# A streaming encoder step on one core: the middle half of each MLP's down product made of seven products of sums instead of eight

## The chip, the cores and the metric

The kernel runs on one core of one Trainium2 chip. The metric is the device time of the program in microseconds. Its engines are TensorE (PE, with its weight loads as PEld), VectorE (DVE), ScalarE (ACT), GpSimd (POOL) and SyncE (SP), which issues the DMAs. Each engine runs its instructions in program order and waits on semaphores for the others.

## What is computed

Two layers over 1056 rows (1024 of a prompt, 32 of a running stream), model width 1024. Layer 0 mixes by spatial gating and a recurrence, layer 1 by a short gated convolution; after each mixer comes the MLP that is changed here:

```python
x = x + rmsnorm(m, p['norm_mix_post'][l])
hn = rmsnorm(x, p['norm_ffn_pre'][l])
f = jnp.square(jax.nn.relu(hn @ p['mlp_up'][l])) @ p['mlp_down'][l]
x = x + rmsnorm(f, p['norm_ffn_post'][l])
```

mlp_up is 1024 x 4096, mlp_down 4096 x 1024, all float32.

## The kernel before

Activations are held transposed: 128 partitions are 128 features, and the 1056 rows are columns, in NT = 3 tiles of TT = 352. A product in float32 is made of three fast matmuls. Each operand is split into a high part (a cast to the short form, on ACT) and a low part (raw minus high, on DVE), and a 128x352 result takes high x high, high weights x low data, low weights x high data, for each of 8 blocks of 128 features: 24 matmuls that accumulate in one PSUM bank (lines 698 to 700, in `unit`). Such a 24 is a *unit*; a *panel* is one load of weights, 1024 x 128, used in 3 units.

`plan` writes down the list of units and of loads. Weights come by SP's DMAs into three rotating places (w_all), each free again when the last unit that used it is done (SP waits on pe_unit). ACT's `high` (line 876) casts them and DVE's `low` (line 1183) subtracts, at the units that high_at and low_at give. 

The MLP runs in four groups. In a group, 8 up panels give 1024 of the 4096 hidden features: DVE's `evacuate` (line 1286) scales and rectifies a PSUM bank into one of three tmp tiles, ACT squares it (937) and casts it to h_hi (939), DVE subtracts into h_lo (`h_low`, 1266). Then 8 down panels multiply these with mlp_down, and DVE adds each bank to f in SBUF (line 1292; the first group's is a copy, 1289). Six PSUM banks go round, so a unit waits for the evacuation six units before. The two other banks (M0, M1) serve norms and transposes, and line 760 is such a small product between units. In the last group f is squared for the norm.

POOL works at the start and in layer 1's mixer (lines 654 to 664), and is idle in the MLPs.

## Time and profile before

| | us |
|---|---|
| median of 3 runs | 2157.8 |
| lowest, highest | 2157.34, 2158.69 |
| span of the profiled execution | 2155.1 |
| PE busy in it | 2146.0 |
| DVE busy | 908.0 |
| ACT busy | 652.9 |
| POOL busy | 100.1 |

The span is measured from the first to the last instruction of the profiled execution; the runs' times contain some 2.7 us more. A matmul's record is about twice as long as its share of PE's time, since the next one starts while it drains: PE's pace is read from starts, not from durations. Weight loads (PEld) overlap the matmuls in the same way.

### The profile page before, as it was taken

Reading aid. Unit: us, or ns where it says so; the run is one execution under the profiler, and the core shown is the slowest. Engines: PE = TensorE matmul, PEld = TensorE weight load, DVE = VectorE, ACT = ScalarE, POOL = GpSimd, SP = SyncE. Lnnn points to the kernel's source line nnn. Section 1 sums busy time; section 2 is a strip of 40 time slices with the busy share of each in tenths; the row PEclk is TensorE's granted clock in tenths of the full one; section 3 lists DMA queues with packets and bytes.
Section 4 is the critical chain, followed back from the end, with each engine's and each line's share of the span. In section 5 each row is a group of like instructions: output and inputs, shape, how many; then the busy total and the mean of one; then the engine's idle time right before and its main releaser. Section 6 shows DMA issues by size and latency. Waiting matters only on the chain.

```text
span 2155.1 us, 31488 instructions
## 1 busy us (share of the span) xinstructions
PE 2146.0 (100%) x13496; PEld 2135.0 (99%) x13496; DVE 908.0 (42%) x1414; ACT 652.9 (30%) x1105; POOL 100.1 (5%) x127
## 2 busy tenths in 40 slices
PE   9999999999999999999999999999999999999998
PEld 9999999999999999999999999999999999999998
DVE  8766367323322322334953333493223223322336
ACT  6673355202301310333511112453013103202332
POOL 2000000000000000000043231000000000000000
PEclk9999999999999999999999999999999999999999
DMA  5111422111111111141311114222111111111142
GB/s 165 35 41 40 139 88 72 50 40 49 50 42 47 49 50 40 49 135 44 120 50 47 43 50 139 67 84 59 42 48 50 49 40 50 50 42 48 50 140 81
DMA packets 208410, 138.65 MB, mean 64 GB/s; under 512 B 6000, under 2 KB 204784, under 8 KB 208272
## 3 DMA queue, kind: packets, MB, share of 16 engines
q1 hardware_dynamic: 207552, 135.51, 20.6%
q8 instruction: 107, 1.75, 0.3%
q10 hardware_dynamic: 720, 1.13, 0.1%
q14 instruction: 31, 0.25, 0.0%
HBM read 119.22 MB, written 17.40 MB: 63 GB/s over the span
## 4 chain that ended last, share of the span: by engine, by line
PE 99%; ACT 1%; DMA 0%; DVE 0%; issue 0%; DVEq 0%; ACTq 0%
PE ps L698 32%; PE ps L700 32%; PE ps L699 32%; PE ps L773 1%; PE ps L801 0%; PE ps L729 0%; PE ps L720 0%; DMA w_all_raw<-in_w_in_even_dram 0%; PE ps L716 0%; PE ps L784 0%; PE ps L760 0%; ACT L1074 0%; ACT L1030 0%; ACT lru L1030 0%; ACT lru L1032 0%; ACT gelu L1074 0%
## 5 line engine op out<-in xcount | busy, mean ns | idle before, releaser
L698 PE MATMUL ps<-x_hi,w_all 128*128 128x352 f32 x2304 | 747.0, 324 | 0.0
L700 PE MATMUL ps<-x_hi,w_all 128*128 128x352 f32 x2304 | 739.1, 321 | 0.0
L699 PE MATMUL ps<-x_lo,w_all 128*128 128x352 f32 x2304 | 739.1, 321 | 0.0
L698 PE MATMUL ps<-h_hi,w_all 128*128 128x352 f32 x1728 | 556.2, 322 | 0.0
L700 PE MATMUL ps<-h_hi,w_all 128*128 128x352 f32 x1728 | 555.2, 321 | 0.0
L699 PE MATMUL ps<-h_lo,w_all 128*128 128x352 f32 x1728 | 555.2, 321 | 0.0
L698 PEld LDWEIGHTS ps<-x_hi,w_all 128*128 128x128 f32 x2304 | 432.4, 188 | 2.7
L699 PEld LDWEIGHTS ps<-x_lo,w_all 128*128 128x128 f32 x2304 | 432.4, 188 | 2.2
L700 PEld LDWEIGHTS ps<-x_hi,w_all 128*128 128x128 f32 x2304 | 432.3, 188 | 0.0
L876 ACT CAST w_all<-w_all_raw 128x1024 fp32r<-128x1024 f32 x166 | 173.5, 1045 | 525.1 <-DMA w_all_raw<-in_mlp_down_dram 324.8
L698 PEld LDWEIGHTS ps<-h_hi,w_all 128*128 128x128 f32 x1728 | 324.5, 188 | 0.3 <-DVE h_lo L1452 0.3
L699 PEld LDWEIGHTS ps<-h_lo,w_all 128*128 128x128 f32 x1728 | 324.5, 188 | 0.0
L700 PEld LDWEIGHTS ps<-h_hi,w_all 128*128 128x128 f32 x1728 | 324.4, 188 | 0.0
L1286 DVE SCALAR_TENSOR_TENSOR tmp<-ps,rstd 128x352 f32<-128x352 f32 x192 | 100.3, 523 | 419.2 <-PE ps L700 419.0
L937 ACT ACTIVATE tmp<-tmp 128x352 f32<-128x352 f32 x192 | 95.7, 498 | 472.4 <-DVE tmp L1286 472.2
L1292 DVE TENSOR_TENSOR f<-ps,f 128x352 f32<-128x352 f32 x144 | 75.3, 523 | 358.6 <-PE ps L700 358.6
L1183 DVE TENSOR_TENSOR w_all<-w_all_raw,w_all 128x1024 fp32r<-128x1024 f32 x166 | 201.8, 1216 | 17.2 <-ACT w_all L876 17.2
L1266 DVE TENSOR_TENSOR h_lo<-tmp,h_hi 128x352 fp32r<-128x352 f32 x192 | 98.9, 515 | 2.3 <-ACT h_hi L939 2.3
L939 ACT CAST h_hi<-tmp 128x352 fp32r<-128x352 f32 x192 | 93.7, 488 | 6.1
L1289 DVE COPY f<-ps 128x352 f32<-128x352 f32 x48 | 25.2, 525 | 138.0 <-PE ps L700 138.0
L698 PE MATMUL ps<-h_hi,x_hi 128*128 128x352 f32 x192 | 61.7, 321 | 0.0
L700 PE MATMUL ps<-h_hi,x_hi 128*128 128x352 f32 x192 | 61.7, 321 | 0.0
(201 smaller groups left out, 1416.0 us busy)
## 6 DMA issues: line engine op xcount, KB each, us to landing
w_all_raw<-in_mlp_up_dram SPq DMA_DIRECT2D x60, 512.0 KB, 3.9
w_all_raw<-in_mlp_down_dram SPq DMA_DIRECT2D x60, 512.0 KB, 3.8
x_save<-f SPq DMA_DIRECT2D x9, 1408.0 KB, 6.0
...
w_all_raw<-in_c_w_in_dram SPq DMA_DIRECT2D x22, 512.0 KB, 3.7
w_all_raw<-in_w_in_even_dram SPq DMA_DIRECT2D x12, 512.0 KB, 3.6
...
w_all_raw<-in_w_out_even_dram SPq DMA_DIRECT2D x6, 512.0 KB, 3.8
```

The costliest lines, as they stand in the source:

```text
L698: nc.tensor.matmul(dst, wh, hi, start=(i == 0), stop=False)
L699: nc.tensor.matmul(dst, wh, lo, start=False, stop=False)
L700: last = nc.tensor.matmul(dst, wl, hi, start=False, stop=(i == KC - 1))
L773: nc.tensor.matmul(ps[:, M0, 0:LT], gate_w[:, g, j, :], xc[j % 2][:, t * LT:(t + 1) * LT], start=True, stop=True).then_inc(gate_pe, 1)
L876: nc.scalar.copy(W[l][0], W[l][2]).then_inc(w_high, 1)
L937: nc.scalar.activation(tmp[n % 3][:, :], tmp[n % 3][:, :], ACT.Square).then_inc(h_sq, 1)
L939: nc.scalar.copy(pt(h_hi, u.m, u.t), tmp[n % 3][:, :]).then_inc(h_high, 1)
L1183: nc.vector.tensor_tensor(lo, raw, hi.bitcast(F32), ALU.subtract).then_inc(w_ready, 1)
L1266: nc.vector.tensor_tensor(pt(h_lo, u.m, u.t), tmp[n % 3][:, :], pt(h_hi, u.m, u.t).bitcast(F32), ALU.subtract).then_inc(h_ready, 1)
L1286: ins = nc.vector.scalar_tensor_tensor(tmp[n % 3][:, :], bank(n), 0.0, scale, ALU.max, ALU.mult)
L1289: ins = nc.vector.tensor_copy(pt(f, m, t), bank(n))
L1292: ins = nc.vector.tensor_tensor(pt(f, m, t), bank(n), pt(f, m, t), ALU.add)
```

## The change

The first and the last 1024 hidden features of each MLP are done as before. The middle 2048 are done in four groups of 512: 4 up panels (12 units of the new kind "us"), then the down product of these 512 features by seven products in Strassen's manner (Winograd's form). Per layer there are 4 such groups, 8 in all.

A down product of a group is cut in 2 x 2 blocks three ways: two output blocks of 128 (a *pair*; 4 pairs make the 1024 outputs), two halves of 256 hidden features, two halves of HT = 528 columns. The weights' blocks are A11, A12, A21, A22, of h they are B11, B12, B21, B22. Sums of weights: S1 = A21 + A22, S2 = S1 - A11, S3 = A11 - A21, S4 = A12 - S2. Sums of h: T1 = B12 - B11, T3 = B22 - B12, T2 = T3 + B11, T4 = B21 - T2. Seven products s1 to s7 stand for eight. Each is 2 column quarters (QT = 264) x 2 feature blocks x 3 matmuls = 12 matmuls of 264 columns, into two banks.

Sums of products aren't made by extra additions: products that share a sum follow one another in the same banks without a fresh start (chain A: s1, s6, s7, s4; C: s5, s3; B: s2), and after each DVE adds the 128x528 state of the chain to the block of f that needs it. So a product of a chain waits until DVE has added the one before it. Chain A of odd pairs uses the banks M0 and M1.

What this puts on the other engines, per group: ACT casts T1 to T4 (8 casts of 528 columns, `t_casts`) and the weight pairs in 7 forms (128x1792 instead of 128x1024); DVE makes T1, T3, T2, the low halves of T3 and T2, one pair's sums (`pair_sums`, 4 instructions of 256 columns), and low parts, those of the third and fourth pair in four pieces of 448 columns; POOL makes T4, the low halves of T1 and T4 and the sums of the other three pairs. A pair's load is one of two DMAs of 256 KB. The rotating places grow from 2 x 1024 to 28 x 128 words a partition. For this small tiles (tail, row_sq and others) move into gaps, h's slot pitch falls from 1088 to 1056 columns, and the DMA scratch is set to 512.

```diff
+SC = 4
+WS = 28 * P
+FORMS = 7 * 2 * P
...
+A11, A12, S3, A22, S1, S2, S4 = range(7)
+PRODUCT = {"s1": (A11, "B11", "A", 0, 0), "s2": (A12, "B21", "B", 0, 0), "s3": (S4, "B22", "C", 0, 1),
+           "s4": (A22, "T4", "A", 1, 0), "s5": (S1, "T1", "C", 1, 1), "s6": (S2, "T2", "A", 0, 1),
+           "s7": (S3, "T3", "A", 1, 1)}
+CHAIN_START = ("s1", "s2", "s5")
+PAIR_ORDER = ([("s1", 0), ("s5", 0), ("s2", 0), ("s3", 0), ("s6", 0), ("s1", 1), ("s7", 0), ("s5", 1), ("s4", 0),
+               ("s6", 1), ("s2", 1), ("s7", 1), ("s3", 1), ("s4", 1)],
+              [("s1", 0), ("s5", 0), ("s6", 0), ("s2", 0), ("s7", 0), ("s3", 0), ("s1", 1), ("s4", 0), ("s5", 1),
+               ("s6", 1), ("s2", 1), ("s7", 1), ("s3", 1), ("s4", 1)])
...
+    def strassen_down(l, row):
+        groups.append(len(units))
+        for h in range(2):
+            pair = []
+            for kind, p in PAIR_ORDER[h]:
+                if p == len(pair):
+                    slot = oldest()
+                    pair.append(load(("mlp_down", l), row, 2 * (2 * h + p), slot, freed[slot], True))
+                    freed[slot] = len(units) + 100
+                use(pair[p], 0, "H", kind, 2 * h + p)
...
-        for g in range(GROUPS):
-            for m in range(4 if g == 0 else 0, 8):
-                panel(("mlp_up", l), 0, 8 * g + m, "X", "up", m)
-            ups.append(len(units) - 1)
-            if g < GROUPS - 1:
-                for m in range(8):
-                    panel(("mlp_down", l), g * D, m, "H", "dn0" if g == 0 else "dn", m)
-            else:
-                out_group(("mlp_down", l), g * D, "dn3")
+        for m in range(4, 8):
+            panel(("mlp_up", l), 0, m, "X", "up", m)
+        for m in range(8):
+            panel(("mlp_down", l), 0, m, "H", "dn0", m)
+        for g in range(2, 6):
+            for j in range(SC):
+                slot = oldest()
+                i = load(("mlp_up", l), 0, SC * g + j, slot, freed[slot])
+                for t in ((0, 1, 2) if j < 2 else (2, 1, 0)):
+                    use(i, t, "X", "us", j)
+            strassen_down(l, SC * g * P)
+        for m in range(8):
+            panel(("mlp_up", l), 0, 3 * KC + m, "X", "up", m)
+        ups.append(len(units) - 1)
+        out_group(("mlp_down", l), 3 * D, "dn3")
...
+        if l.pair:
+            gs, p = max(g for g in GROUP if g <= l.first), l.col // 2
+            high_at.append(gs + (-5, -3, 7, 12)[p])
+            low_at.append([[gs - 4], [gs - 2], [gs + 8 + i for i in range(4)], [gs + 14 + i for i in range(4)]][p])
...
+        chain = PRODUCT[u.kind][2]
+        a = {"A": (0, M0)[u.m % 2], "B": 4, "C": 2}[chain]
+        return (a, a + 1)
...
-        w_all = place("w_all", [P, 6, D], F32R)
-        w_all_raw = place("w_all_raw", [P, 6, D], F32, at_w)
+        w_all = place("w_all", [P, 3, WS], F32R)
...
+        def pair_sums(engine, eng, l, signal, before):
+            w = W[l][2]
+            a11, a12, a21, a22, s1, s2, s4 = [w[:, 2 * b:2 * b + 2, :] for b in (A11, A12, S3, A22, S1, S2, S4)]
+            eng.wait_ge(w_in[LOADS[l].slot], landed[l])
+            engine.tensor_tensor(s1, a21, a22, ALU.add).then_inc(signal, 1)
+            eng.wait_ge(signal, before + 1)
+            engine.tensor_tensor(a21, a11, a21, ALU.subtract).then_inc(signal, 1)
+            engine.tensor_tensor(s2, s1, a11, ALU.subtract).then_inc(signal, 1)
+            eng.wait_ge(signal, before + 3)
+            engine.tensor_tensor(s4, a12, s2, ALU.subtract).then_inc(signal, 1)
...
+                elif LOADS[l].pair:
+                    name, i = LOADS[l].name
+                    r, m = LOADS[l].row, LOADS[l].col
+                    for h in range(2):
+                        src = A[name][i][r:r + SC * P, (m + h) * P:(m + h + 1) * P]
+                        sp.dma_start(W[l][2][:, SC * h:SC * h + SC, :], src.rearrange("(k p) n -> p k n", p=P)
+                                     ).then_inc(w_in[slot], 16)
...
+            def t4_add(q, c):
+                pool.wait_ge(h_ready, index[GROUP[q] - (4, 1)[c]] + 1)
+                pool.wait_ge(t_sum, 4 * q + 2 * c + 2)
+                raw = t_form(h_lo_raw, 4, c)
+                nc.gpsimd.tensor_tensor(raw, raw, t_form(h_lo_raw, 2, c), ALU.subtract).then_inc(t4_sum, 1)
+            def t4_low(q, c):
+                pool.wait_ge(t_high, 8 * q + (5, 8)[c])
+                raw = t_form(h_lo_raw, 4, c)
+                nc.gpsimd.tensor_tensor(t_form(h_lo, 4, c), raw, t_form(h_hi, 4, c).bitcast(F32), ALU.subtract
+                                        ).then_inc(t4_ready, 1)
+            def strassen_group(q):
+                t1_low(q, 0)
+                t1_low(q, 1)
+                pair_sums(nc.gpsimd, pool, PAIRS[q][0], w_sum_p, 12 * q)
+                for c in range(2):
+                    t4_add(q, c)
+                    t4_low(q, c)
+                pair_sums(nc.gpsimd, pool, PAIRS[q][2], w_sum_p, 12 * q + 4)
+                pair_sums(nc.gpsimd, pool, PAIRS[q][3], w_sum_p, 12 * q + 8)
...
+                if form == "B11":
+                    pe.wait_ge(h_ready, index[gs - 7] + 1)
+                if form in ("B21", "B22"):
+                    pe.wait_ge(h_ready, index[gs - 1] + 1)
+                if form == "T1":
+                    pe.wait_ge(t1_ready, 2 * q + 2)
+                if form == "T2":
+                    pe.wait_ge(t23_ready, 4 * q + 3)
+                if form == "T3":
+                    pe.wait_ge(t23_ready, 4 * q + 4)
+                if form == "T4":
+                    pe.wait_ge(t4_ready, 2 * q + 2)
...
+                bank_free(n)
+                for i, b in enumerate(banks(n)):
+                    dst = ps[:, b, 0:QT]
+                    for c in range(2):
+                        wh, wl = [W[u.load][which][:, 2 * a + c, :] for which in range(2)]
+                        hi, lo = moving(h_hi, form, c, i), moving(h_lo, form, c, i)
+                        nc.tensor.matmul(dst, wh, hi, start=(c == 0 and u.kind in CHAIN_START), stop=False,
+                                         skip_group_check=True)
+                        nc.tensor.matmul(dst, wh, lo, start=False, stop=False, skip_group_check=True)
+                        last = nc.tensor.matmul(dst, wl, hi, start=False, stop=(c == 1), skip_group_check=True)
+                last.then_inc(pe_unit, 1)
...
+                for o0, o1, half, c0 in up_pieces(u):
+                    nc.scalar.activation(square_place(u, half, c0, o1 - o0), sq_tmp(n)[:, o0:o1], ACT.Square
+                                         ).then_inc(h_sq if split else h_high, 1)
+                if not split:
+                    return
+                act.wait_ge(h_sq, sq_no[n] + len(up_pieces(u)))
+                for o0, o1, half, c0 in split:
+                    last = nc.scalar.copy(cols(h_hi, u.m, half * HT + c0, o1 - o0), square_place(u, half, c0, o1 - o0))
+                last.then_inc(h_high, 1)
...
+                    if s in (-9, -6):
+                        c = (-9, -6).index(s)
+                        act.wait_ge(h_ready, index[gs - (10, 7)[c]] + 1)
+                        t_cast(1, c)
+                    if s in (-5, -1):
+                        c = (-5, -1).index(s)
+                        act.wait_ge(t_sum, 4 * q + 2 * c + 1)
+                        t_cast(3, c)
+                        act.wait_ge(t_sum, 4 * q + 2 * c + 2)
+                        t_cast(2, c)
+                    if s in (-3, 0):
+                        c = (-3, 0).index(s)
+                        act.wait_ge(t4_sum, 2 * q + c + 1)
+                        t_cast(4, c)
...
+            def low_part(l, i, parts):
+                dve.wait_ge(w_high, l + 1)
+                c0, c1 = [j * FORMS // parts for j in (i, i + 1)]
+                hi, lo, raw = [w.rearrange("p k n -> p (k n)")[:, c0:c1] for w in W[l]]
+                last = nc.vector.tensor_tensor(lo, raw, hi.bitcast(F32), ALU.subtract)
+                if i == parts - 1:
+                    last.then_inc(w_ready, 1)
...
+            def t32_add(q, c):
+                t3 = t_form(h_lo_raw, 3, c)
+                dve.wait_ge(h_ready, index[GROUP[q] - (5, 2)[c]] + 1)
+                nc.vector.tensor_tensor(t3, t3, b12_raw(c), ALU.subtract).then_inc(t_sum, 1)
+                dve.wait_ge(t_sum, 4 * q + 2 * c + 1)
+                nc.vector.tensor_tensor(t_form(h_lo_raw, 2, c), t3, b11_raw(c), ALU.add).then_inc(t_sum, 1)
+            def t_low(q, i, c):
+                dve.wait_ge(t_high, 8 * q + {3: (3, 6), 2: (4, 7)}[i][c])
+                if i == 2:
+                    dve.wait_ge(t4_sum, 2 * q + c + 1)
+                nc.vector.tensor_tensor(t_form(h_lo, i, c), t_form(h_lo_raw, i, c), t_form(h_hi, i, c).bitcast(F32),
+                                        ALU.subtract).then_inc(t23_ready, 1)
+            def strassen_before(n):
+                if UNITS[n - 1].kind == "us":
+                    halves_low(n - 1)
+                for q, gs in enumerate(GROUP):
+                    if n == gs - 4:
+                        t32_add(q, 0)
+            def strassen_after(n):
+                for q, gs in enumerate(GROUP):
+                    s = n - gs
+                    if s == -3:
+                        t_low(q, 3, 0)
+                        pair_sums(nc.vector, dve, PAIRS[q][1], w_sum_d, 4 * q)
+                    if s == -2:
+                        t_low(q, 2, 0)
+                    if s == -1:
+                        t32_add(q, 1)
+                    if s == 1:
+                        t_low(q, 2, 1)
+                    if s == 2:
+                        t_low(q, 3, 1)
...
-                if u.kind in ("dn", "dn3"):
-                    dve.wait_ge(evac_d, evac_no[n - 48] + 1)
+                if u.kind in STRASSEN:
+                    a, fm, c0, c1 = banks(n)[0], *f_blocks(n)
+                    dve.wait_ge(evac_d, evac_no[f_writer[n]] + 1)
+                    sums = f[:, fm * TOK + c0:fm * TOK + c1].rearrange("p (q n) -> p q n", q=2)
+                    ins = nc.vector.tensor_tensor(sums, ps[:, a:a + 2, 0:QT], sums, ALU.add)
...
+                    dynamic_dma_scratch_size=512)
```

DVE, at the entry of the down product of the middle features. Before, from the last up units of a group to its first down panels (h_lo is the low half, w_all<-w_all_raw the weights' low part):

```order
L1266 TENSOR_TENSOR h_lo<-tmp_56,h_hi 128x352
L1183 TENSOR_TENSOR w_all<-w_all_raw,w_all 128x1024
L1286 SCALAR_TENSOR_TENSOR tmp_58<-ps,rstd 128x352
L1266 TENSOR_TENSOR h_lo<-tmp_57,h_hi 128x352
L1292 TENSOR_TENSOR f<-ps,f 128x352
L1266 TENSOR_TENSOR h_lo<-tmp_58,h_hi 128x352
L1292 TENSOR_TENSOR f<-ps,f 128x352
L1183 TENSOR_TENSOR w_all<-w_all_raw,w_all 128x1024
L1292 TENSOR_TENSOR f<-ps,f 128x352 x3
```

Now, from four units before a Strassen group (the first two rows are T3 and T2 of the first half of columns; 128x1792 are a pair's low parts, 528 with h_hi low halves of T3 and T2, 128x256 a pair's sums):

```order
L1567 TENSOR_TENSOR h_lo_raw<-h_lo_raw,h_hi_raw 128x528
L1569 TENSOR_TENSOR h_lo_raw<-h_lo_raw 128x528
L1618 SCALAR_TENSOR_TENSOR tmp_58<-ps,rstd 128x352
L1463 TENSOR_TENSOR w_all<-w_all_raw,w_all 128x1792
L1557 TENSOR_TENSOR h_lo<-h_lo_raw,h_hi 128x352
L1618 SCALAR_TENSOR_TENSOR tmp_56<-ps,rstd 128x352
L1576 TENSOR_TENSOR h_lo<-h_lo_raw,h_hi 128x528
L471 TENSOR_TENSOR w_all_raw<-w_all_raw 128x256
L473 TENSOR_TENSOR w_all_raw<-w_all_raw 128x256
L474 TENSOR_TENSOR w_all_raw<-w_all_raw 128x256
L476 TENSOR_TENSOR w_all_raw<-w_all_raw 128x256
L1557 TENSOR_TENSOR h_lo<-h_lo_raw,h_hi 128x352
```

Between the same evacuations there stand the forms and their low halves, twice the weight columns, and four short sums.

DVE, right behind, across the first products of the group (1626 adds a chain's state to f):

```order
L1576 TENSOR_TENSOR h_lo<-h_lo_raw,h_hi 128x528
L1463 TENSOR_TENSOR w_all<-w_all_raw,w_all 128x1792
L1557 TENSOR_TENSOR h_lo<-h_lo_raw,h_hi 128x176 x2
L1618 SCALAR_TENSOR_TENSOR tmp_58<-ps,rstd 128x352
L1567 TENSOR_TENSOR h_lo_raw<-h_lo_raw,h_hi_raw 128x528
L1569 TENSOR_TENSOR h_lo_raw<-h_lo_raw 128x528
L1557 TENSOR_TENSOR h_lo<-h_lo_raw,h_hi 128x352
L1626 TENSOR_TENSOR f<-ps,f 128x528 x2
L1576 TENSOR_TENSOR h_lo<-h_lo_raw,h_hi 128x528
L1626 TENSOR_TENSOR f<-ps,f 128x528
L1576 TENSOR_TENSOR h_lo<-h_lo_raw,h_hi 128x528
L1626 TENSOR_TENSOR f<-ps,f 128x528 x6
```

The low half of the last up unit (first row of h_lo with 352 columns) stands ahead of the first product's addition, and T2's and T3's low halves between additions.

POOL, in the first MLP. Before, nothing stands between the mask of layer 0 and the pads of layer 1:

```order
L612 TENSOR_SCALAR soft<-soft 128x4
L632 MEMSET ws_t 64x4x64
L637 MEMSET cp_96 128x2
L637 MEMSET cp_99 128x2
L654 TENSOR_TENSOR cp_96<-tmp_57,cg_95 128x352
```

Now there is a block like this for each group (784 is T1's low half, 471 to 476 a pair's sums, 791 T4, 796 its low half):

```order
L784 TENSOR_TENSOR h_lo<-h_lo_raw,h_hi 128x528 x2
L471 TENSOR_TENSOR w_all_raw<-w_all_raw 128x256
L473 TENSOR_TENSOR w_all_raw<-w_all_raw 128x256
L474 TENSOR_TENSOR w_all_raw<-w_all_raw 128x256
L476 TENSOR_TENSOR w_all_raw<-w_all_raw 128x256
L791 TENSOR_TENSOR h_lo_raw<-h_lo_raw 128x528
L796 TENSOR_TENSOR h_lo<-h_lo_raw,h_hi 128x528
L791 TENSOR_TENSOR h_lo_raw<-h_lo_raw 128x528
L796 TENSOR_TENSOR h_lo<-h_lo_raw,h_hi 128x528
L471 TENSOR_TENSOR w_all_raw<-w_all_raw 128x256
```

The second and third pair of such a block follow with eight more instructions on w_all_raw.

## Rows read from the trace of the kernel before

**Rows 1.** Page, parts 1, 2 and 4, in part.

```profile
PE 2146.0 (100%) x13496; PEld 2135.0 (99%) x13496; DVE 908.0 (42%) x1414; ACT 652.9 (30%) x1105; POOL 100.1 (5%) x127
...
PEclk9999999999999999999999999999999999999999
...
PE 99%; ACT 1%; DMA 0%; DVE 0%; issue 0%; DVEq 0%; ACTq 0%
```

**Rows 2.** Stretch: us; busy (x) of PE, PEld, DVE, ACT, POOL; clock; DMA.

```profile
588.00:680.00 92.00, 92.00 (x581) 92.00 (x580) 22.53 (x35) 9.38 (x10) 0.00 (x0) 1.00 0.16 47
...
600.00:800.00 200.00, 200.00 (x1263) 200.00 (x1262) 56.89 (x93) 41.79 (x66) 0.00 (x0) 1.00 0.17 48
```

**Rows 3.** PE in order of time (start us, us, engine, line), in an MLP.

```profile
1000.08 0.32 PE L699 MATMUL ps<-h_lo,w_all 128*128 128x352 f32 x1
...
1001.98 0.32 PE L699 MATMUL ps<-h_lo,w_all 128*128 128x352 f32 x1
```

**Rows 4.** PE in order of time, around an 11-column matmul of two passes.

```profile
1017.06 0.28 PE L760 MATMUL ps<-x_old,quads 128*128 128x11 f32 x2
...
1017.44 0.32 PE L699 MATMUL ps<-h_lo,w_all 128*128 128x352 f32 x1
```

**Rows 5.** PEld, the weight loads, in the same stretch.

```profile
1017.17 0.19 PEld L698 LDWEIGHTS ps<-h_hi,w_all 128*128 128x128 f32 x1
1017.28 0.19 PEld L699 LDWEIGHTS ps<-h_lo,w_all 128*128 128x128 f32 x1
```

**Rows 6.** Line 826, 128-column transposes near the end.

```profile
L826 PE MATMUL ps<-ident,x_old x16: 270/272/273, 2143.6 to 2145.2; 128*128 128x128 f32 x16
```

**Rows 7.** PE in order of time, from a panel's last matmuls to the next's.

```profile
594.78 0.32 PE L700 MATMUL ps<-h_hi,w_all 128*128 128x352 f32 x1
594.94 0.32 PE L698 MATMUL ps<-h_hi,w_all 128*128 128x352 f32 x1
```

**Rows 8.** DVE in the same stretch.

```profile
595.14 0.53 DVE L1292 TENSOR_TENSOR f<-ps,f 128x352 f32<-128x352 f32 x1 [2.88 <-PE ps L700]
595.58 1.21 DVE L1183 TENSOR_TENSOR w_all<-w_all_raw,w_all 128x1024 fp32r<-128x1024 f32 x1
```

**Rows 9.** DVE groups by shape (busy us, mean ns | idle before).

```profile
L1183 DVE TENSOR_TENSOR w_all<-w_all_raw,w_all 128x1024 fp32r<-128x1024 f32 x166 | 201.8, 1216 | 17.2 <-ACT w_all L876 17.2
...
L1266 DVE TENSOR_TENSOR h_lo<-tmp,h_hi 128x352 fp32r<-128x352 f32 x192 | 98.9, 515 | 2.3 <-ACT h_hi L939 2.3
L1292 DVE TENSOR_TENSOR f<-ps,f 128x352 f32<-128x352 f32 x144 | 75.3, 523 | 358.6 <-PE ps L700 358.6
...
L1427 DVE SCALAR_TENSOR_TENSOR mixed<-ps,vecs,bias_bc 128x512 f32<-128x512 f32 x8 | 6.0, 748 | 5.3 <-PE ps L801 5.3
...
L1228 DVE TENSOR_TENSOR x_old<-x_old 128x704 f32<-128x704 f32 x6 | 5.3, 892 | 0.2
```

**Rows 10.** ACT groups by shape.

```profile
L876 ACT CAST w_all<-w_all_raw 128x1024 fp32r<-128x1024 f32 x166 | 173.5, 1045 | 525.1 <-DMA w_all_raw<-in_mlp_down_dram 324.8 <-DMA w_all_raw<-in_mlp_up_dram 125.8 <-DMA w_all_raw<-in_c_w_in_dram 55.4
...
L939 ACT CAST h_hi<-tmp 128x352 fp32r<-128x352 f32 x192 | 93.7, 488 | 6.1
```

**Rows 11.** POOL groups by shape.

```profile
L664 POOL TENSOR_TENSOR h_lo<-cy,h_hi 128x352 fp32r<-128x352 f32 x24 | 23.7, 986 | 15.9 <-ACT h_hi L1147 15.2 <-DVE tmp L1324 0.7
```

**Rows 12.** DVE in order of time, odd layer.

```profile
1133.71 1.22 DVE L1183 TENSOR_TENSOR w_all<-w_all_raw,w_all 128x1024 fp32r<-128x1024 f32 x1
```

**Rows 13.** POOL in order of time, same stretch.

```profile
1130.14 0.95 POOL L654 TENSOR_TENSOR cp<-tmp,cg 128x352 f32<-128x352 f32 x1 [11.75 <-DVE tmp L1324]
1133.94 1.79 POOL L654 TENSOR_TENSOR cp<-tmp,cg 128x352 f32<-128x352 f32 x1 [2.85 <-DVE tmp L1324]
```

**Rows 14.** Line 1248, DVE, two SBUF inputs: min/median/max ns.

```profile
L1248 DVE SCALAR_TENSOR_TENSOR x_lo<-f,vecs,x_hi x96: 544/576/1127, 6.2 to 1440.6; 128x352 fp32r<-128x352 f32 x96
```

**Rows 15.** DMA issues by source (KB each, median us to landing).

```profile
w_all_raw<-in_mlp_down_dram SPq DMA_DIRECT2D x60, 512.0 KB, 3.8
```

240 lines of the change are left out of this document (188 added, 52 removed).

## Prediction

> **What bounds the kernel now.** I read the page's busy shares first, then the chain that ended last: PE is busy 2146.0 of 2155.1 us, the chain lies on PE for 99%, and the granted clock is 1.00 throughout, which is the 2.4 GHz level [rows 1]. So the sum is made over PE's matmuls, and every other engine matters only where it makes PE wait. The table by stretch then shows how much room the others have: in a stretch of down products (588 to 680 us) DVE works 22.5 of 92 us, ACT 9.4, POOL nothing [rows 2].
>
> **What one matmul costs.** The unit is the distance from one start to the next, not the 0.32 us of a record, since records overlap. Twelve steps take 1001.98 - 1000.08 = 1.90 us, 158.3 ns each [rows 3]; 200 us with 1263 matmuls give 158.4 [rows 2]. At 2.4 GHz 352 columns are 146.7 ns, so 11.7 ns come on top. Each matmul brings its own weight load (as many loads as matmuls [rows 1]), which runs beside the matmul before it.
>
> **What the change removes on PE.** The middle half of each down product was, per layer, 2 blocks of 8 panels, each panel 3 token tiles of 8 row blocks with 3 matmuls (high by high, high by low, low by high): 2 x 2 x 8 x 3 x 8 x 3 = 2304 matmuls of 352 columns. 2304 x 0.1584 = 364.9 us.
>
> **What it adds on PE.** 8 groups x 4 pairs x 7 products x 12 = 2688 matmuls of 264 columns: 709,632 columns against 811,008, seven eighths. No row shows a 264-column matmul. Bounds: nothing but its columns, 110.0 ns; in proportion to the 352-column step, 118.8; with the same 11.7 ns on top, 121.7; upper end, no shorter than a step of 352 columns, 158.4. A second floor is the weight load: from the first of two 11-column passes to the matmul after the next, 0.38 us hold these two and one full step, so (0.38 - 0.158) / 2 = 0.11 us for a pass that streams almost nothing [rows 4]; the loads there stand 0.11 us apart [rows 5]; 128-column transposes come every (2145.2 - 2143.6) / 15 = 0.107 us [rows 6]. That floor is under 110 + 11.7 but close to 110, so it takes nothing off and forbids much less than 0.11. I take 121.7 ns: the 11.7 ns come once for each matmul and its load, and the step is the same in a stretch where DVE works a quarter of the time (92.00 us, 581 matmuls, 158.3 ns) as in the mixed 200 us [rows 2], so it is no contention that would shrink with the reading. 2688 x 0.1217 = 327.1 us. PE alone: 327.1 - 364.9 = **-37.8 us**; with 118.8 ns -45.6, with 112 ns -63.9. The break-even is 364.9 / 2688 = 135.8 ns.
>
> By the Trainium skill ("TensorE: Matmul & The Clock Gate", "Back-to-back issue gap") a step is the columns at 2.4 GHz plus about 2.5 ns, so a 264-column step would be 112.5 ns; the 352-column step would be 149.2, where the trace has 158.3. The measurement decides; what it gives is the first rival.
>
> **Evacuations and chains on DVE.** A product is 12 matmuls, 12 x 0.1217 = 1.46 us, and its 128x528 sum must be added to f before a later product of the same chain may accumulate on it. In the tightest places one other product stands between (s5 to s3, s6 to s7, s7 to s4). Today the sum starts 0.20 us after the first matmul of the next panel (594.94 to 595.14 [rows 7, 8]). A 128x352 one from PSUM takes 523 ns, a 128x512 one 748 [rows 9]; on that slope 528 columns take 0.77 us. It ends 0.97 us into the next product, 0.49 us before it is needed. The cover is thin but there. DVE pieces come in between: the low parts, now 128x448 four at a time. A 128x704 with SBUF inputs takes 892 ns and a 128x352 515 [rows 9], so 448 take about 0.62; and an instruction starts 0.09 us before the one ahead has ended (595.14 + 0.53 against 595.58 [rows 8]). 0.77 + 0.62 - 0.18 = 1.21 us in a product of 1.46. I cost them at nothing.
>
> **Work moved beside PE, per group (12 up units of 24 x 0.1584 = 3.80 us, then 28 products, 86.5 us).** DVE: 12 evacuations and 12 halves (12 x 1.04 = 12.5), 28 sums (21.6), four up panels' low parts (4.9), four pairs' low parts (128x1792 each, 1216 ns per 1024 [rows 9]: 2.1, so 8.5), ten 528-column forms (0.70 each: 7.0), one pair's sums (4 x 0.41 = 1.6): 56 us, 65%. ACT: about 30 us, from 1045 ns per 1024 and 488 per 352 [rows 10]. POOL: 6 x 528 and 12 x 256 columns at 0.95 to 0.99 us per 352 [rows 11, 13]: 17 to 19 us. No engine is a bound by its sum.
>
> **The group's entry is where it can fail.** Product three of a group (s2) reads the last up panel's h; it starts 2 x 1.46 = 2.92 us after the last up unit's end. From that unit's end: evacuation starts after 0.2 and ends at 0.7, ACT squares and casts it by 1.7, DVE makes the two sums T3 and T2 in between (0.7 to 2.1), then the low half, ready at 2.6. That leaves 0.3 us, if DVE comes to this unit with nothing left over. It does not: in the three up units before it (11.4 us) it has two low parts of 2.1 us, each waiting for ACT's 1.7 us cast, and the first of these for POOL's, the second for DVE's own sums, for 11 to 12 us of work in a row. The second cast can't start before the load has landed, 3.8 us after the slot is free [rows 15], and the sums (1.6 us) are done. POOL makes it later: a DVE instruction with two SBUF inputs and a POOL one do not run together. POOL's 352 columns take 0.95 us alone and 1.79 when DVE's 1.22 us instruction has begun 0.23 us before [rows 12, 13], and DVE's line 1248 goes from 576 to 1127 ns once [rows 14]. I put one such collision (0.5 to 1.4 us) into each entry: low half ready at 3.0 to 4.6 us instead of 2.6, so PE waits 0.1 to 1.7 us. I take 1.0 us in each of 8 groups, **+8 us**, bounds 0 and 24 (3 us each, two collisions and the late load). The Trainium skill ("SBUF — State Buffer", "Who interferes with whom") says the same of the two engines, a lock for the whole instruction; the trace agrees, and the price here is by the rows.
>
> The third and fourth pairs of a group are loaded while products run. The fourth's slot comes free at product 9; landing 3.8 us [rows 15], POOL's four sums 2.8 to 3.8, ACT's cast 1.8, in all 8.4 to 9.4 us after product 9 ends, where DVE's first piece of it is due 6 x 1.46 + 0.97 = 9.7 us after. Cost nothing, at most 0.5 us a group (in the 24). DMA moves as many bytes as before; the smaller DMA scratch moves nothing that PE waits for, and the moved small tiles cost nothing.
>
> **Sum.** On the span: 2155.1 - 37.8 + 8 = 2125.3; the median of the runs is 2.7 above the span, so **2128 us**.
>
> **Rivals.** (1) *Short step*: 264 columns take 112 to 118.8 ns. For it: nothing shows that the 11.7 ns are fixed. Against: a pass needs 0.11 us for its load anyway [rows 4 to 6], and no step of 352 is near 149. With 112 ns and 8 us of waits 2157.8 - 63.9 + 8 = 2102, with 118.8 2120. Chance 0.20. (2) *Waits eat the gain*: DVE and POOL collide at several entries and at the fourth pair, 2 to 4 us a group: 2157.8 - 37.8 + 16 to 32 = 2136 to 2152. For it: the 0.3 us of room; against: PE's banks let two products run before the late half. Chance 0.20. (3) *Slower*: DVE cannot keep pace within the chains. Each of the 224 products would wait for the sum two before it; from 37.8 / 224 = 0.17 us per product beyond the entry's waits the change loses. That needs sum and piece to take 1.63 us where I have 1.21, or a 264-column step over 135.8 ns. At 0.25 us per product: 2157.8 - 37.8 + 8 + 56 = 2184. Against: it needs a third more DVE time in every product than the rows give, and POOL works in fewer than half of them. Chance 0.07. (4) *It does not come out shorter*, waits and step just cancel, 2153 to 2162: 0.03.
>
> **How the numbers follow.** Forecast (2128, from 2120 to 2136) 0.50, rivals 0.20, 0.20, 0.07, 0.03. The range leaves out the lower half of (1) and all of (3), (4) and the top of (2): **2108 to 2148**. A measurement of this kernel tells 0.2% (4 us) from no change. Faster 0.90, same 0.03, slower 0.07.
>
> **What would show it.** Right: 2688 matmuls of 264 columns at 121 to 123 ns from start to start; PE's idle or late starts at the third product of each group, ended by the low half on DVE; nothing at the loads. Wrong on the step: another distance inside a product. Wrong on the waits: gaps at s7, s3 or s4 (chains), or at the first products after a pair change (w_all of the fourth pair), or POOL records near 2 us everywhere. The forecast is wrong as a whole if the granted clock leaves 1.00 in the groups.

## The result and the profile after

The changed kernel takes 2183.1 us (median; 2180.9 to 2183.3) against 2157.8 before: ratio 1.0114, 95% interval 1.010 to 1.013. It is **slower by 25 us**, where 2128 was forecast. The profiled execution's span is 2181.2 us against 2155.1, so the difference of the spans, 26.1 us, is the one to explain (the profiled run of the changed kernel took 1.8 us more than its span, where the kernel before has 2.7).

The page of the changed kernel, parts 1, 2 and 4, answers to [rows 1]:

```profile
PE 2158.2 (99%) x13880; PEld 2146.0 (98%) x13880; DVE 1125.6 (52%) x1702; ACT 704.1 (32%) x1201; POOL 240.1 (11%) x271
...
PEclk9999999999999999999999999999999999999999
...
PE 86%; issue 10%; DVE 1%; ACT 1%; DMA 0%; POOL 0%; DVEq 0%; ACTq 0%; SPq 0%; POOLq 0%
```

PE is still the bound and the clock still granted. There are 384 matmuls more (2304 of 352 columns out, 2688 of 264 in), and DVE and POOL work more, as forecast. Nothing here tells where 26 us came from. The groups by line do, once the ones that the change did not touch are read too (part 5; mean ns is the last number before the second bar):

```profile
L876 PE MATMUL ps<-x_hi,w_all 128*128 128x352 f32 x2304 | 759.5, 330 | 0.0
...
L876 PE MATMUL ps<-h_hi,w_all 128*128 128x352 f32 x960 | 310.8, 324 | 0.0
...
L922 PE MATMUL ps<-h_hi,w_all 128*128 128x264 f32 x896 | 256.4, 286 | 13.6 <-issue 9.0
...
L1626 DVE TENSOR_TENSOR f<-ps,f 128x528 f32<-128x528 f32 x224 | 157.4, 705 | 90.9 <-PE ps L925 89.3
```

The same matmul of 352 columns has records of 324 ns when it reads h and of 330 when it reads x (the first two rows). A record is not a step, so the steps (start to next start) are read from PE in order of time. First a stretch of layer 1's mixer, whose matmuls read x, then products of the second Strassen group of layer 0:

```profile
1200.00 0.33 PE L876 MATMUL ps<-x_hi,w_all 128*128 128x352 f32 x1
...
1202.00 0.33 PE L876 MATMUL ps<-x_hi,w_all 128*128 128x352 f32 x1
```

```profile
640.57 0.29 PE L922 MATMUL ps<-h_hi,w_all 128*128 128x264 f32 x1
...
642.03 0.29 PE L922 MATMUL ps<-h_hi,w_all 128*128 128x264 f32 x1
```

Twelve matmuls on x take 2.00 us, 166.7 ns each, where [rows 3] had 158.3 for the same shape on h; twelve of 264 columns take 1.46 us, 121.7 ns each, just as forecast. The counts in windows of the changed kernel show where the slow step holds (columns as in [rows 2]):

```profile
505.00:535.00 30.00, 30.00 (x192) 30.00 (x191) 10.55 (x19) 9.96 (x22) 5.17 (x6) 1.00 0.14 41
595.00:625.00 30.00, 30.00 (x182) 30.00 (x181) 9.66 (x17) 8.80 (x18) 3.35 (x3) 1.00 0.16 47
...
1120.00:1300.00 180.00, 180.00 (x1081) 180.00 (x1081) 58.57 (x87) 24.07 (x45) 51.35 (x51) 1.00 0.15 45
```

A window counts the records that straddle its edges too, so a short one reads about 1% low. The up panels that follow a down panel of 352 columns (505 to 535) come out at 30/192 = 156 ns (158.3 from start to start), those that follow a Strassen group (595 to 625) at 165 (166.7), layer 1's mixer at 166.5. The last stretch in the kernel before:

```profile
1120.00:1300.00 180.00, 180.00 (x1139) 180.00 (x1138) 61.76 (x93) 23.96 (x45) 52.31 (x50) 1.00 0.16 48
```

1139 against 1081 matmuls in 180 us, with the granted clock at 1.00 in both. DVE's busy time is 61.8 and 58.6 us, POOL's 52.3 and 51.4, so the others do not work more beside the slow step.

**The account.** The step of a matmul is the time from its start to the next one's. For 352 columns the steps of 150 to 200 ns are summed; the few others add up to 23 us on x and 3 us on h in both kernels and are left out. For 264 columns a step over 140 ns counts as late. Over both traces this gives, for the difference of 26 us:

| steps of PE | before | after | difference, us |
|---|---|---|---|
| 352 columns, on x | 7415 x 158.5 ns = 1175.4 us | 7416 x 164.8 ns = 1222.2 us | +46.8 |
| 352 columns, on h | 5747 x 158.9 = 913.3 | 3443 x 159.2 = 548.2 | -365.1 |
| 264 columns | none | 2656 x 121.8, and 32 late ones, 20.9 us in all = 344.4 | +344.4 |
| sum | | | +26.1 |

Of the 7416 steps on x, 5694 take 166.6 ns and the others 158.7. At 121.8 ns the 32 late steps would have been 3.9 us, so 17.0 us of them are waits. Without waits and without the slow step the seven products would have brought 365.1 - 327.4 = 37.7 us, against 37.8 forecast.

**The waits** on PE in the changed kernel (line waited for, us in total, times, longest):

```profile
PE ps L922 <- issue: 9.0, 6, 1.5
PE ps L922 <- DVE h_lo L1557: 4.6, 2, 2.3
```

All eight are at the third product, s2. From the last start before it to its own first start they are 2.45 us longer than a step in the first group of a layer and 1.64 to 1.67 in the other three. This is that entry in the second group of layer 0, PE first, then DVE, then POOL (start us, us, engine, line; the bracket is idle time and its releaser):

```profile
643.36 0.28 PE L925 MATMUL ps<-h_hi,w_all 128*128 128x264 f32 x1
645.12 0.36 PE L922 MATMUL ps<-h_hi,w_all 128*128 128x264 f32 x1 [1.48 <-issue]
```

```profile
634.29 1.61 DVE L1576 TENSOR_TENSOR h_lo<-h_lo_raw,h_hi 128x528 fp32r<-128x528 f32 x1
635.83 0.41 DVE L471 TENSOR_TENSOR w_all_raw<-w_all_raw 128x256 f32<-128x256 f32 x1
636.27 1.43 DVE L473 TENSOR_TENSOR w_all_raw<-w_all_raw 128x256 f32<-128x256 f32 x1
...
639.29 0.70 DVE L1576 TENSOR_TENSOR h_lo<-h_lo_raw,h_hi 128x528 fp32r<-128x528 f32 x1
640.27 2.03 DVE L1463 TENSOR_TENSOR w_all<-w_all_raw,w_all 128x1792 fp32r<-128x1792 f32 x1 [0.28 <-ACT w_all L1109]
...
642.71 0.52 DVE L1618 SCALAR_TENSOR_TENSOR tmp<-ps,rstd 128x352 f32<-128x352 f32 x1
...
644.50 0.52 DVE L1557 TENSOR_TENSOR h_lo<-h_lo_raw,h_hi 128x352 fp32r<-128x352 f32 x1
```

```profile
634.02 1.32 POOL L791 TENSOR_TENSOR h_lo_raw<-h_lo_raw 128x528 f32<-128x528 f32 x1 [6.51 <-DVE h_lo L1557]
636.08 1.34 POOL L796 TENSOR_TENSOR h_lo<-h_lo_raw,h_hi 128x528 fp32r<-128x528 f32 x1 [0.74 <-ACT h_hi L1190]
```

s2 starts 0.10 us after the low half of the last up unit (line 1557) has ended at 645.02, so DVE releases it, though the profile calls it issue. DVE comes to that unit with work left over: the low parts at 640.27 (2.03 us) hold the last unit's evacuation until 642.71, 2.1 us after the group's first matmul started (640.57) and not 0.2. DVE had been set back 1.9 us before: line 1576 takes 1.61 us beside POOL's 791 (0.70 alone, at 639.29), and line 473 1.43 beside POOL's 796 (0.43 alone, in e4_t4_late below).

**The clock** falls once in the eight groups, in layer 0's first, behind the gap of 2.45 us:

```profile
548.60:553.00 4.40, 2.10 (x19) 1.93 (x17) 4.37 (x8) 2.44 (x6) 0.04 (x1) 1.00 0.40 119
553.00:560.00 7.00, 7.00 (x45) 7.00 (x46) 5.00 (x7) 0.98 (x3) 5.92 (x6) 0.76 0.00 1
```

PE ran 2.1 of 4.4 us, then some 16 matmuls took 220 ns instead of 122, at the 1.2 GHz level, 1.6 us in all (part of the 17.0). The same gap in layer 1's first group was followed by none.

### The profile page after: what moved, and what is told of

Its sections match the earlier page's. It is cut to its first block, busy times and chain, and to the rows that moved or that the text cites. A ratio compares the mean times of both kernels' runs of the same rounds, so it can differ in the third digit from the quotient of the medians.

```text
span 2181.2 us, 33137 instructions
## 1 busy us (share of the span) xinstructions
PE 2158.2 (99%) x13880; PEld 2146.0 (98%) x13880; DVE 1125.6 (52%) x1702; ACT 704.1 (32%) x1201; POOL 240.1 (11%) x271
## 4 chain that ended last, share of the span: by engine, by line
PE 86%; issue 10%; DVE 1%; ACT 1%; DMA 0%; POOL 0%; DVEq 0%; ACTq 0%; SPq 0%; POOLq 0%
PE ps L876 24%; PE ps L877 23%; PE ps L878 23%; PE ps L922 5%; PE ps L925 5%; PE ps L924 5%; PE ps L996 1%; PE ps L1024 0%; ACT w_all L1109 0%; DVE h_lo L1557 0%; PE ps L952 0%; PE ps L943 0%; DMA w_all_raw<-in_w_in_even_dram 0%; PE ps L939 0%; DVE w_all L1463 0%
## 5 line engine op out<-in xcount | busy, mean ns | idle before, releaser
L876 PE MATMUL ps<-x_hi,w_all 128*128 128x352 f32 x2304 | 759.5, 330 | 0.0
L878 PE MATMUL ps<-x_hi,w_all 128*128 128x352 f32 x2304 | 751.6, 326 | 0.0
L1109 ACT CAST w_all<-w_all_raw 128x1024 fp32r<-128x1024 f32 (+1 forms) x166 | 194.5, 1172 | 470.0 <-DMA w_all_raw<-in_mlp_up_dram 141.4
L876 PE MATMUL ps<-h_hi,w_all 128*128 128x352 f32 x960 | 310.8, 324 | 0.0
L878 PE MATMUL ps<-h_hi,w_all 128*128 128x352 f32 x960 | 307.9, 321 | 0.0
L877 PE MATMUL ps<-h_lo,w_all 128*128 128x352 f32 x960 | 307.9, 321 | 0.0
L922 PE MATMUL ps<-h_hi,w_all 128*128 128x264 f32 x896 | 256.4, 286 | 13.6 <-issue 9.0
L925 PE MATMUL ps<-h_hi,w_all 128*128 128x264 f32 x896 | 255.5, 285 | 0.0
L924 PE MATMUL ps<-h_lo,w_all 128*128 128x264 f32 x896 | 255.4, 285 | 0.0
L1626 DVE TENSOR_TENSOR f<-ps,f 128x528 f32<-128x528 f32 x224 | 157.4, 705 | 90.9 <-PE ps L925 89.3
L922 PEld LDWEIGHTS ps<-h_hi,w_all 128*128 128x128 f32 x896 | 169.6, 189 | 15.0 <-issue 15.0
L877 PEld LDWEIGHTS ps<-h_lo,w_all 128*128 128x128 f32 x960 | 180.6, 188 | 0.0
L876 PEld LDWEIGHTS ps<-h_hi,w_all 128*128 128x128 f32 x960 | 180.2, 188 | 0.3 <-DVE h_lo L1789 0.3
L878 PEld LDWEIGHTS ps<-h_hi,w_all 128*128 128x128 f32 x960 | 180.0, 188 | 0.0
L1456 DVE TENSOR_TENSOR w_all<-w_all_raw,w_all 128x1024 fp32r<-128x1024 f32 x134 | 162.8, 1215 | 17.2 <-ACT w_all L1109 17.2
L924 PEld LDWEIGHTS ps<-h_lo,w_all 128*128 128x128 f32 x896 | 169.6, 189 | 0.0
L925 PEld LDWEIGHTS ps<-h_hi,w_all 128*128 128x128 f32 x896 | 169.4, 189 | 0.0
## 6 DMA issues: line engine op xcount, KB each, us to landing
x_old<-x_save SPq DMA_DIRECT2D x9, 1408.0 KB, 12.7
```

Of the source, the lines that this page charges most:

```text
L876: nc.tensor.matmul(dst, wh, hi, start=(i == 0), stop=False)
L877: nc.tensor.matmul(dst, wh, lo, start=False, stop=False)
L878: last = nc.tensor.matmul(dst, wl, hi, start=False, stop=(i == KC - 1))
L922: nc.tensor.matmul(dst, wh, hi, start=(c == 0 and u.kind in CHAIN_START), stop=False, skip_group_check=True)
L924: nc.tensor.matmul(dst, wh, lo, start=False, stop=False, skip_group_check=True)
L925: last = nc.tensor.matmul(dst, wl, hi, start=False, stop=(c == 1), skip_group_check=True)
```

## Experiments on the slow step

**Theory L**: where the buffers lie in SBUF makes the matmuls on x slow, whatever work runs. **Rival P**: the products of sums do it (POOL and DVE traffic, larger pieces). In the table, "distance" is from the first byte of x_hi to that of w_all in a partition, worked out from the storage plan; steps are means over all 352-column matmuls on x, late ones left out. "T4 late" is the edit of e7_both, further below.

| kernel | products | distance, bytes | steps on x, ns | of these at 163 or more | median, us |
|---|---|---|---|---|---|
| before | 8 | 177,280 | 158.5 | 148 | 2157.8 |
| e1_scratch | 8 | 177,280 | 158.6 | 226 | 2158.2 |
| e5_w2048 | 8 | 179,328 | 158.7 | 255 | 2158.2 |
| e6_pitch | 8 | 177,280 | 158.6 | 222 | 2158.6 |
| e2_layout | 8 | 175,232 | 161.6 | 2815 | 2180.6 |
| e9_hpitch | 8 | 175,232 | 161.5 | 2788 | 2180.7 |
| e10_layout128 | 8 | 175,360 | 160.1 | 166 | 2169.9 |
| after | 7 | 175,232 | 164.8 | 5694 | 2183.1 |
| e8_w64 | 7 | 175,296 | 160.1 | 270 | 2155.3 |
| e3_wpad | 7 | 175,360 | 160.2 | 194 | 2153.2 |
| e12_x128 (T4 late) | 7 | 175,232 | 164.8 | 5674 | 2176.3 |
| e13_m64 (T4 late) | 7 | 175,168 | 160.1 | 349 | 2148.0 |
| e15_w160 (T4 late) | 7 | 175,328 | 160.1 | 133 | 2147.5 |
| e11_both_w192 (T4 late) | 7 | 175,424 | 160.1 | 335 | 2148.0 |
| e7_both (T4 late) | 7 | 175,360 | 160.1 | 176 | 2143.9 |

**e1_scratch**: of the change, the DMA scratch alone, in the kernel before.

```diff
-    nc = _bacc.Bacc("TRN2", target_bir_lowering=False, num_devices=1)
+    nc = _bacc.Bacc("TRN2", target_bir_lowering=False, num_devices=1,
+                    dynamic_dma_scratch_size=512)
```

> The kernel before with one line changed: the DMA scratch is 512 bytes, so that x, h, f and the weights' places all start 15,872 bytes lower. In the changed kernel 5,694 of the 7,416 unchanged matmuls with x as the moving operand come 166.6 ns apart, in the kernel before 158.4. Theory L (the layout in SBUF decides the step): some of that returns here if the base alone matters, at most 7,416 x 8.2 ns = 61 us: between 2158 and 2215 us. Theory P (the step is set by what PE did just before, the Strassen products and their late starts, not by addresses): 2158 us and 158.4 ns, as before.

Measured: ratio 1.0001 (0.9991 to 1.001). Neither the scratch nor a shift of everything by 15,872 bytes does anything.

**e2_layout**: the whole storage plan of the changed kernel, with the old list of units and eight products. From its plan, against the kernel before:

```diff
-TS = TOK + 32
+TS = TOK
...
+        at_byte[0] += 64
         at_f = at_byte[0]
...
-        at_byte[0] += 128
+        at_byte[0] += 64
         at_w = at_byte[0]
-        w_all = place("w_all", [P, 6, D], F32R)
+        w_all = place("w_all", [P, 3, WS], F32R)
...
```

> The changed kernel's whole layout in SBUF (scratch, pitch of h, places of the weights, small tiles) with the unit list of the kernel before, eight products and no sums. Theory L: the x steps are at 166.6 ns in most of the program, in which no Strassen product stands, 2158 + 47 to 61 us = 2205 to 2219. Theory P: 158.4 ns and 2158 us.

Measured: 2180.6, ratio 1.0105 (1.009 to 1.012), 22.7 us more on x's steps with **no product of sums in the program**, though less than half of the 47 to 61 us that were expected. Its row for layer 1's mixer:

```profile
1120.00:1300.00 180.00, 180.00 (x1082) 180.00 (x1081) 59.55 (x90) 22.63 (x43) 50.79 (x52) 1.00 0.16 45
```

1082 matmuls, as in the changed kernel. P is out as the cause. It keeps a part: here the MLP's up panels stay fast, and all of them follow 352-column matmuls on h; in the changed kernel those after Strassen groups are slow too, which raises 2815 slow steps to 5694 and gives the other 24 us of the 46.8.

**e3_wpad** and **e8_w64**: the changed kernel with 128 or 64 bytes more ahead of w_all and of what lies behind it (the edit of e3_wpad; e8_w64 has 128 in place of 192).

```diff
-        at_byte[0] += 64
+        at_byte[0] += 192
         at_w = at_byte[0]
```

> The changed kernel with 128 bytes more ahead of the weights' places (and of all that follows), nothing else. Theory L, if the distance between x and the weights matters modulo a small power of two: another share of slow x steps than 5,694 of 7,416, and a time between 2136 (none slow) and 2197 (all). If only coarse distances matter, or theory P: the same shares and 2183.

> The changed kernel with 64 bytes more ahead of the weights' places (128 gave x steps of 160.0 ns, none gave 166.7 in most stretches). If any distance but the changed kernel's own frees the step, x steps near 160 and 2153 us; if the step follows the distance in steps of 128 bytes, 166.7 ns and 2183 us; in between, a third value.

Measured: 2153.2 (0.9974, 0.9964 to 0.9983) and 2155.3 (0.9989, 0.998 to 0.9999). The steps of 166.6 are gone and steps of 160.1 to 160.2 ns in their place, 12 to 13 us over the 158.5 of the kernel before. In e3_wpad:

```profile
1120.00:1300.00 180.00, 180.00 (x1127) 180.00 (x1126) 61.77 (x93) 23.95 (x45) 52.19 (x50) 1.00 0.16 47
```

```profile
PE ps L922 <- DVE h_lo L1557: 17.0, 8, 2.1
```

34 us of steps come back, but with faster up panels DVE has less time before each entry, s2 is 2.3 us late in all eight groups, and in four of these some 16 matmuls at the 1.2 GHz level follow. The waits grow from 17.0 to 25.1 us. How many groups lose the clock seems to change from run to run of the same program: the ten runs of e3_wpad lie between 2148.2 us, at a mean granted clock of 0.999, and 2154.7, at 0.996, and four groups at 1.6 us each are 6.4 us. Only the longest of them has a trace.

**e5_w2048** and **e6_pitch**, on the kernel before with the small scratch: w_all 2048 bytes further from x (the distance is then 3200 modulo 4096, as in the changed kernel), and its places 10,240 bytes apart instead of 8192.

```diff
-        at_byte[0] += 128
+        at_byte[0] += 128 + 2048
...
```

```diff
-        w_all = place("w_all", [P, 6, D], F32R)
+        w_all = place("w_all", [P, 3, 2560], F32R)
...
```

> The kernel before with the DMA scratch of 512 bytes (as in the run with only that) and the weights' places 2,048 bytes higher. That makes the distance from x to the weights 179,328 bytes, which leaves 3,200 modulo 4,096, as in the changed kernel (175,232 bytes); before it leaves 1,152. Theory D (that distance modulo 4,096 sets the slow step): x steps of 166.6 ns in the mixers and in layer entries, about 2,800 of 7,416 as with the changed layout, 2158 + 23 = 2181 us. If the distance matters only in smaller moduli, 2158 us and 158.4 ns.

> The kernel before with the DMA scratch of 512 bytes and a pitch of 10,240 bytes from place to place of the weights instead of 8,192, so that the second place stands half a 4,096 further, as with the 14,336 bytes of the changed kernel. Theory D in the form that the pitch of the places brings the slow step: 2181 us. In the form that the base distance does: 2158 us.

Measured: ratios 1.0000 (0.9991 to 1.0009) and 1.0002 (0.9993 to 1.0011), and steps of 158.7 and 158.6. Both of my guesses at a rule fell.

**e9_hpitch**, on the kernel before with the small scratch: of the new storage plan the base, the pitch of h and the gaps, so that w_all begins where it does in the changed kernel, but with its old six places.

```diff
-TS = TOK + 32
+TS = TOK
...
+        at_byte[0] += 64
         at_f = at_byte[0]
...
-        at_byte[0] += 128
+        at_byte[0] += 64
         at_w = at_byte[0]
...
```

> The kernel before, its eight products and its six weight places 8192 bytes apart, with the 512-byte scratch and h stored at a pitch of 1056 instead of 1088 columns, so that w_all begins at byte 175,872, just where it begins in the changed kernel. It parts the two things of the layout that are left: where w_all lies against x, and the larger places in it. If the address decides (theory A): some thousands of the 7415 steps of the matmuls that read x take 166.6 ns, as in the run with the whole new layout (2815 of them), and the time is 2175 to 2182. If the larger places are needed as well (theory W): steps of 158.5 and 2158.

Measured: 2180.7, ratio 1.0107 (1.0093 to 1.0121), as e2_layout. The larger places are not needed. Nor do the buffers behind w_all (tmp, rstd and others) decide: they lie 18,432 bytes nearer to it here than in e2_layout, and the slow steps are 2788 and 2815.

```profile
1120.00:1300.00 180.00, 180.00 (x1082) 180.00 (x1081) 59.07 (x90) 22.62 (x43) 50.79 (x51) 1.00 0.15 45
```

**e10_layout128**: e2_layout with 128 bytes more ahead of w_all (`+= 192`).

> The run with the whole new layout and the old list of eight products (2180.6, 2815 steps of the matmuls that read x at 166.6 ns), with 128 bytes more between f and w_all, as in the run that freed the changed kernel. Theory A (the offset of w_all against x decides, whatever the products): no steps of 166 ns are left, all x steps are 158 to 160 ns, and the time is 2158 to 2171 (7415 steps at 160.1 instead of 158.5 are 11.9 us over 2158). If the products were needed for the pad to work: 2180.

Measured: 2169.9, ratio 1.0057 (1.0041 to 1.0072); steps of 160.1, 12.4 us more than before in x's steps and 12.1 in the time. The pad works in the same way with eight products:

```profile
1120.00:1300.00 180.00, 180.00 (x1127) 180.00 (x1126) 60.64 (x92) 26.03 (x49) 55.16 (x55) 1.00 0.16 48
```

**e12_x128**: e7_both (below) with the 128 bytes ahead of x_hi instead, so that all buffers move together.

```diff
+        at_byte[0] += 128
         at_x_hi = at_byte[0]
...
-        at_byte[0] += 192
+        at_byte[0] += 64
         at_w = at_byte[0]
```

> The fastest version so far (2143.9), with the 128 bytes not between f and w_all but ahead of x_hi: everything moves up by 128 bytes together, w_all lies at the same byte 176,000 as in that version, and the distance from x to w_all is again that of the changed kernel (175,232). Theory R (the distance decides): x steps of 166.6 ns in most stretches are back, 5700 x 6.6 ns = 38 us over 2143.9, so about 2175 to 2190. Theory P (the place of w_all by itself decides): 160.1 ns and 2144. That moving all of the kernel before by 15,872 bytes did nothing speaks for R.

Measured: 2176.3, ratio 1.0086 (1.0072 to 1.0099); 5674 steps of 166.6 are back. w_all lies on the same byte in e7_both and here, so it is **how w_all lies against the activations**, not where it lies:

```profile
1120.00:1300.00 180.00, 180.00 (x1082) 180.00 (x1081) 58.73 (x90) 23.61 (x45) 50.50 (x52) 1.00 0.15 45
```

**e13_m64**, **e15_w160** and **e11_both_w192**: e7_both with 0, 160 and 256 bytes between f and w_all instead of 192.

> The fastest version so far (2143.9, distance from x to w_all 175,360) with no gap between f and w_all: distance 175,168, 64 bytes below that of the changed kernel. If 175,232 is a single bad distance: x steps of 160.1 ns and 2144, or of 158.5 ns and 2132. If the slow step holds for all distances up to 175,232: steps of 166.6 ns and 2176, as in the run with x moved along.

> The fastest version so far with 32 bytes less ahead of w_all: distance 175,328, 96 bytes above that of the changed kernel and no multiple of 64. Both neighbours, 175,296 and 175,360, gave 160.1 ns. If steps follow the distance in units of 64 bytes or more: 160.1 ns and 2144. If a start within a 64-byte unit costs something: more than 160.1 ns, up to the 166.6 ns of the changed kernel and 2176.

> The fastest version so far (2143.9: 128 bytes ahead of w_all, both T4 low parts late) with 64 bytes more ahead of w_all, 256 in all. Its x steps are 160.1 ns where the kernel before has 158.5. If the step follows the offset of w_all in pieces of 64 bytes, it can come out at 158.4 (7416 steps x 1.6 ns = 11.9 us less: 2132), stay at 160.1 (2144), or go to 166.6 (+48: 2192). I expect 160.1 and 2144, since offsets of 64 and of 128 bytes gave the same step.

Measured: 2148.0, 2147.5 and 2148.0 (in the order of the headings) with steps of 160.1 in all three. 175,232 is the only one of the six distances between 175,168 and 175,424 with the step of 166.6; none of them gives 158.5. They are 4 us behind e7_both because the matmuls on h step 160.0 ns in them and 159.0 in it (3443 x 1.0 = 3.4 us): h has its own good and bad offsets.

## Experiments on the wait

The theory of the prediction: s2 waits for DVE, which POOL sets back, since the two do not run together on SBUF. If so, moving POOL's T4 low parts behind the entry must shorten the wait by the collision that it removes. **e4_t4_late**, on the changed kernel:

```diff
-                for c in range(2):
-                    t4_add(q, c)
-                    t4_low(q, c)
+                t4_add(q, 0)
+                t4_add(q, 1)
+                t4_low(q, 0)
+                t4_low(q, 1)
```

> The changed kernel with one pair of lines in another order on POOL: the low half of the first T4 comes behind the second T4, so that it no longer runs beside the pair's sums on DVE at the entry of a group, one of whose four takes 1.43 us there instead of 0.41. Theory of the prediction (the third product waits for work queued on DVE, which POOL's instructions delay): the wait there falls by about 1.0 us in each of 8 groups, from 2.5 us to 1.5 in the first group of a layer and from 1.7 to 0.7 in the others, 2183 - 8 = 2175 us, a little less where the x steps are slow. Rival (the wait is set by ACT's cast or the load, whatever POOL does): no change, 2183.

Measured: 2178.9, ratio 1.0097 (1.0082 to 1.0112). The wait at s2 fell by 1.00 us in every group (2.45 to 1.45, 1.65 to 0.65), because the instruction of line 473 is 0.43 us again with nothing of POOL beside it:

```profile
633.82 0.43 DVE L473 TENSOR_TENSOR w_all_raw<-w_all_raw 128x256 f32<-128x256 f32 x1
```

Of the 8 us expected, half came: POOL now works later in the group, and the starts at the fifth and the seventh product are 0.25 and 0.22 us late. 17.0 us of waits became 12.5, and the kernel 4.2 us faster.

**e7_both**: e3's 128 bytes, and T4's low parts held back until DVE's T3 and T2 are done, with the third pair's low parts one product later.

```diff
-                for c in range(2):
-                    t4_add(q, c)
-                    t4_low(q, c)
+                t4_add(q, 0)
+                t4_add(q, 1)
+                pool.wait_ge(t23_ready, 4 * q + 4)
+                t4_low(q, 0)
+                t4_low(q, 1)
...
-            low_at.append([[gs - 4], [gs - 2], [gs + 8 + i for i in range(4)], [gs + 14 + i for i in range(4)]][p])
+            low_at.append([[gs - 4], [gs - 2], [gs + 9 + i for i in range(4)], [gs + 14 + i for i in range(4)]][p])
...
-        at_byte[0] += 64
+        at_byte[0] += 192
         at_w = at_byte[0]
```

> The changed kernel with the 128 bytes ahead of the weights' places, both low halves of T4 on POOL behind DVE's last form of the group, and the low parts of the third pair one product later. The 128 bytes alone gave 2153.2 us, with a wait of 2.30 us at the third product of each group, and 16 matmuls at half the clock behind it in half of the groups. If POOL's instructions beside DVE's four sums are what delays the third product: a wait of about 1.3 us there and none at products five and seven, no fall of the clock, 2153.2 - 8 - 6 = 2139 us. Rival (what is moved only waits elsewhere): 2147 to 2153 us.

Measured: **2143.9 us, ratio 0.9935 (0.992 to 0.9949)**, faster than both kernels. s2 waits 1.28 us instead of e3's 2.30, the fifth and seventh products wait for nothing, and the clock stays granted in all eight groups. It is 5 us above the 2139 expected. From the list of waits:

```profile
PE ps L924 <- issue: 8.9, 8, 1.1
...
PE ps L924 <- DVE w_all L1465: 0.5, 2, 0.3
```

The second line is new: the later low parts of the third pair make the fifteenth product 0.16 to 0.45 us late. Account against the kernel before: matmuls on x +12.7 us, on h -365.7, 264 columns +340.1 with 13.5 of waits among them, in all -12.9; the spans differ by 13.5 us, the medians by 13.9. The two moves, POOL's and the third pair's, were not tried apart.

## Why the prediction was wrong

**The step that failed** is the half sentence "the smaller DMA scratch moves nothing that PE waits for, and the moved small tiles cost nothing". It was put down as housekeeping and priced at zero, without a row. It is true of the scratch (e1) and false of what the room was used for. The plan moved w_all to where it lies 175,232 bytes from x_hi, and 5694 matmuls which no line of the change touches step 166.6 instead of 158.5 ns: **+46.8 us, more than the gain**. The prediction took the step of a 352-column matmul as a constant of the chip, after seeing 158.3 and 158.4 in two places. The trace of before held a hint: 148 of its 7415 steps on x are of 166 ns, 142 of them in the first 200 us. None of the rivals had a mechanism outside the changed lines.

**The 264-column step** was right to 0.1 ns: 121.8 against 121.7. The fixed 11.7 ns come once for each matmul; rival 1 is out. The Trainium skill ("TensorE: Matmul & The Clock Gate", "Back-to-back issue gap") gives columns at 2.4 GHz plus about 2.5 ns as the gap of an isolated matmul and says that in a stream of weight loads and matmuls both set the spacing. The prediction left that condition out when it worked an estimate of 112.5 ns for 264 columns from it. No step of these kernels follows the formula: 264 columns step 121.8 ns, 352 columns 158.3 and not 149.2.

**The entry's wait** had the right place, releaser and cause, but the term was mis-sized: 8 us in the sum, 17.0 measured (14.8 of it at the first start of s2, 0.6 at its second, 1.6 the half clock). I put one collision of about 1 us into each entry; there are two in the leftover work, at lines 1576 (+0.91) and 473 (+1.00). Only the second was taken away, in e4_t4_late, and the wait fell by 1.00; what the first adds to the wait was not tested. In the first group of each layer 0.8 us come on top, where the up panels ahead are fast: by my estimate four units of 24 matmuls at 8.3 ns less leave DVE 0.8 us less. The same estimate fits e3_wpad, whose up panels are 6.6 ns faster ahead of every group: 96 x 6.6 ns = 0.63 us on 1.65, and it has 2.3 in all eight. The measured 1.65 is at the top of the stated 0.1 to 1.7, 2.45 beyond it. That range does not follow from its own terms: 2.6 us and a collision of 0.5 to 1.4 make 3.1 to 4.0, a wait of 0.2 to 1.1. That the clock could fall after such a gap was not in the sum, though the prediction named a fall in the groups as a sign that it is wrong as a whole; it came in one group and cost 1.6 us. That POOL and DVE hold each other up agrees with the Trainium skill ("SBUF — State Buffer", "Who interferes with whom"): DVE's 1.61 us against 0.70 at line 1576, 1.43 against 0.43 at line 473.

**The chains** cost nothing, as forecast: sums of 528 columns take 0.71 us where I had 0.77, and beyond the entry no product starts late by more than 0.01 us in the changed kernel, the half clock left out. The third and fourth pairs cost nothing there either. DVE's load was 56 us a group by my sum and is 53 to 54 in the trace, and rival 3 did not happen. With only the waits as measured the time would be 2157.8 - 37.7 + 17.0 = 2137, inside the range; the layout put it outside.

**What stays open.** The runs show that the position of w_all against x and h decides, not the base, the places' pitch, a distance modulo 4096, or the products. They do not show the rule: 175,232 is slow, 175,168 and 175,296 to 175,424 give 160.1, and 177,280 and 179,328 give 158.5. All kernels with 158.5 have the old pitch of h and all with 160.1 the new one, so it is open whether the pitch or the distance parts these two. x and h always moved together, so the distance to x_hi alone, to x_lo or to h is not told apart. Nor is it shown why a stretch on x that follows 352-column matmuls on h keeps the fast step in the bad layout.
